# Decode attention of a hybrid decoder step: keys scored in five rounds of four blocks instead of four groups of five, the fold through two banks, score rows turned through a bank of their own

## The reference

```python
H_SB = H_FOX = 5; HEAD_DIM = 64; DEC_BATCH = 8; DEC_SEQ = 8; PAST_LEN = 4096; PAGE_SIZE = 128

# stick-breaking: q (B,T,H,d), k/v (B,S,H,d)
z = (jnp.einsum('bthd,bshd->bhts', qb, k) * scale).astype(F32)
mask = k_pos[None, :] < pb[:, None]
ln1m = jnp.where(mask, jax.nn.log_sigmoid(-z), 0.0)
rc = lax.cumsum(ln1m, axis=3, reverse=True)
excl = jnp.concatenate([rc[..., 1:], jnp.zeros_like(rc[..., :1])], axis=-1)
a = jnp.where(mask, jnp.exp(jax.nn.log_sigmoid(z) + excl), 0.0)
out = jnp.einsum('bhts,bshd->bthd', a, v)

# forgetting attention
s = (jnp.einsum('bthd,bshd->bhts', qb, k) * scale).astype(F32)
s = s + c_q - c_k                                  # cumulative log forget
p = jax.nn.softmax(jnp.where(mask, s, -jnp.inf), axis=-1)
out = jnp.einsum('bhts,bshd->bthd', p, v)

# the past keys and values come out of paged pools
g = pool[page_table]                               # 32 pages of 128 rows per sequence
```

## Time and profile before

| | |
|---|---|
| median of three runs | 3724.05 us |
| the profiled execution | 3717.23 us, of which the traced span is 3715.7 us |
| PE busy in the span | 3302.2 us (89%) |
| DVE, ACT, POOL busy | 1365.7, 937.0, 596.1 us |
| mean granted TensorE clock | 0.912 of full speed |
| scoring matmuls (L1043) | 896 + 384 instructions, 40 per sequence over 32 sequences |
| key loads of 160 KB issued by SP in decode | 248 + 240 per kind |
| value loads of 160 KB issued by POOL | 480 per kind |

### The profile page before, as it was taken

The page is one execution under the profiler, slowest core; times in us unless marked ns, Lnnn a source line. Parts: engine busy times, 40 slices in busy tenths (PEclk is TensorE's granted clock), DMA queues, the critical chain, the costliest instruction groups (busy, mean ns, idle before and its releaser), DMA issues. The chain is left out here.

```text
span 3715.7 us, 67414 instructions
## 1 busy us (share of the span) xinstructions
PE 3302.2 (89%) x25160; PEld 2100.0 (57%) x25160; DVE 1365.7 (37%) x3002; ACT 937.0 (25%) x1682; POOL 596.1 (16%) x1090
## 2 busy tenths in 40 slices
PE   6999999888899878789989999888889997887998
PEld 4566666555576645444445566655556674554443
DVE  3235055444242534412133151664432244442121
ACT  2012122343122433212020122334322253331110
POOL 0000000144200024410000000003540101542000
PEclk9999955899998899989999999889999997998999
DMA  5011100588411179821021111028871204985102
GB/s 173 18 38 45 44 1 1 172 296 289 151 42 62 35 243 299 289 91 50 29 95 34 32 35 38 21 93 266 293 242 44 75 1 151 310 290 191 55 30 71
DMA packets 268656, 439.67 MB, mean 118 GB/s; under 512 B 48817, under 2 KB 216402, under 8 KB 268338
## 3 DMA queue, kind: packets, MB, share of 16 engines
q1 hardware_dynamic: 205810, 239.96, 20.2%
q0 software_dynamic: 55744, 189.25, 15.4%
q10 hardware_dynamic: 6912, 7.87, 0.6%
HBM read 410.28 MB, written 26.65 MB: 118 GB/s over the span
## 5 line engine op out<-in xcount | busy, mean ns | idle before, releaser
L794 PE MATMUL ps<-W,xT 128*128 128x320 f32 (+7 forms) x5120 | 1479.0, 464 | 11.5 <-DVEq L442 11.5
L794 PEld LDWEIGHTS ps<-W,xT 128*128 128x128 f32 (+1 forms) x5120 | 854.2, 183 | 583.3 <-issue 288.3
L676 POOL DMA_DIRECT2D branch<-in_cache_sb_v_dram x480 | 258.1, 538 | 703.6 <-issue 662.7
L676 POOL DMA_DIRECT2D branch<-in_cache_fox_v_dram x480 | 258.1, 538 | 599.3 <-issue 557.1
L1426 ACT ACTIVATE branch<-ps 128x512 f32<-128x512 f32 x288 | 165.7, 595 | 384.0 <-PE ps L1021 379.7
L1021 PE MATMUL ps<-C,W 128*128 128x128 f32 x1280 | 197.7, 299 | 72.5 <-DMA W<-in_cache_fox_k_dram 23.8
L934 PE MATMUL ps<-branch 64*128 64x512 f32 (+7 forms) x480 | 243.6, 643 | 19.7 <-POOLq L442 19.7
L1021 PE MATMUL ps<-C,branch 128*128 128x128 f32 x1280 | 190.6, 290 | 59.7 <-DMA branch<-in_cache_fox_k_dram 16.6
L1106 PE MATMUL ps<-branch 128*8 128x64 f32 x9920 | 180.9, 233 | 58.6 <-DMA branch<-in_cache_fox_v_dram 30.9
L1021 PEld LDWEIGHTS ps<-C,W 128*128 128x128 f32 x1280 | 149.8, 150 | 139.8 <-issue 61.6
L1043 PE MATMUL ps<-branch,work 128*32 128x512 f32 x896 | 224.4, 613 | 0.7
(11 more groups left out here) (237 smaller groups left out, 3364.0 us busy)
## 6 DMA issues: line engine op xcount, KB each, us to landing
branch<-in_cache_sb_v_dram POOLq DMA_DIRECT2D x480, 160.0 KB, 4.4
branch<-in_cache_fox_v_dram POOLq DMA_DIRECT2D x480, 160.0 KB, 4.0
W<-in_cache_sb_k_dram SPq DMA_DIRECT2D x248, 160.0 KB, 3.3
W<-in_cache_fox_k_dram SPq DMA_DIRECT2D x248, 160.0 KB, 3.4
branch<-in_cache_sb_k_dram SPq DMA_DIRECT2D x240, 160.0 KB, 4.5
branch<-in_cache_fox_k_dram SPq DMA_DIRECT2D x240, 160.0 KB, 4.2
W<-in_w_in_dram SPq DMA_DIRECT2D x14, 1280.0 KB, 6.3
W<-in_w_in_dram SPq DMA_DIRECT2D x9, 1536.0 KB, 7.1
```

The source lines that it names most:

```text
L676: pool.dma_start(ringV[:, g % 2, p * DA:(p + 1) * DA], cache[L, bass.ds(pg, 1)].rearrange("a s h d -> s (a h d)"))\
L794: ins = pe.matmul(out, src[:, k, t * P:t * P + R], W[i % 2][:, k, a:z], start=(k == 0), stop=(k == kc - 1), **place)
```

## The change

A scoring now takes four blocks, 4r to 4r + 3, all in one bank (2 or 3 by the round's parity), so there are five rounds of scoring and five turns of rows, one for each. All rows are turned through bank 6, each after the drain of the one before it. The fold of sb goes in three parts through banks 5, 7 and 5, and the addition on DVE is in three parts as well; the fox fold uses bank 5 for the maximum and 7 for the spread. DVE takes block 8 also (ACT no longer does). The orders on PE, ACT and DVE are written anew: weigh 3 moves from behind block 7 to behind block 3, weigh 0, 1 and 2 stand as shown below. The loads are not touched.

```diff
 SLOTS = 8
+ROUNDS = BLOCKS // 4
-DVE_BLOCKS = (2, 3, 11, 13, 15, 17, 19)
+DVE_BLOCKS = (2, 3, 8, 11, 13, 15, 17, 19)
+FOLD_BANKS = (5, 7, 5)
...
-                def score(b, g):
+                def score(b, r):
-                    n = 5 * g + 4
+                    n = 4 * r + 3
...
-                    if not is_first(b) or g >= 2:
-                        pe.wait_ge(s["rows_out"], 5 * b + g - (1 if g >= 2 else 0) if g else 5 * b)
-                    if g == 1 and not is_first(b):
-                        pe.wait_ge(s["soft_ready"], b)
-                    for kk in range(5):
-                        bank = 3 if kk == 4 else (5 if g % 2 else 2)
-                        q = 32 * (g if kk == 4 else kk)
-                        ins = pe.matmul(ps[q:q + 32, bank, :], q_now[:, kk, :], kT_d[(5 * g + kk) % SLOTS],
-                                        start=True, stop=True, tile_position=(0, q), skip_group_check=True)
+                    if not is_first(b) or r >= 2:
+                        pe.wait_ge(s["rows_out"], ROUNDS * b + r - 1)
+                    for a in range(4):
+                        n = 4 * r + a
+                        ins = pe.matmul(ps[32 * a:32 * a + 32, 2 + r % 2, :], q_now[:, n % 5, :], kT_d[n % SLOTS],
+                                        start=True, stop=True, tile_position=(0, 32 * a), skip_group_check=True)
...
-                def turn_rows(b, j):
+                def turn_rows(b, r):
+                    pe.wait_ge(s["rows_out"], ROUNDS * b + r + 1)
+                    if not is_first(b) or r >= 1:
+                        pe.wait_ge(s["z_drained"], ROUNDS * b + r)
                     for m in range(4):
-                        ins = pe.transpose(ps[:, 6 + j % 2, m * P:(m + 1) * P],
-                                           z_rows[:, 2 if j == 4 else j % 2, m * P:(m + 1) * P], ident)
+                        ins = pe.transpose(ps[:, 6, m * P:(m + 1) * P], z_rows[:, r % 3, m * P:(m + 1) * P], ident)
...
-                def fold(b):
+                def fold(b, c):
                     if kind == "sb":
                         pe.wait_ge(s["sum_ready"], b + 1)
+                        if not is_first(b) or c == 2:
+                            pe.wait_ge(s["fold_taken"], 3 * b + c - 1 if c else 3 * b)
+                        cols = slice(c * 440, c * 440 + 440)
+                        out = ps[:, FOLD_BANKS[c], 0:440]
+                        pe.matmul(out, const("earlier"), soft[:, cols], start=True, stop=False)
+                        pe.matmul(out, const("negones"), later[:, cols], start=False, stop=True)\
+                            .then_inc(s["expo_ready"], 1)
```

The order on PE:

```diff
                 def sequence(b, before=None, two_before=None):
-                    turn_blocks(b, range(0, 5))
+                    turn_blocks(b, range(0, 4))
+                    if two_before is not None:
+                        weigh(two_before, 3)
+                    turn_blocks(b, range(4, 8))
+                    score(b, 0)
                     if before is not None:
                         fold_first(before)
-                    turn_blocks(b, range(5, 8))
-                    if two_before is not None:
-                        weigh(two_before, 3)
-                    score(b, 0)
-                    turn_blocks(b, range(8, 10))
+                    turn_blocks(b, range(8, 12))
+                    score(b, 1)
                     if before is not None:
-                        fold(before)
-                    turn_blocks(b, range(10, 13))
+                        fold(before, 0)
+                        fold(before, 1)
                     turn_rows(b, 0)
-                    score(b, 1)
-                    turn_blocks(b, range(13, 15))
+                    if before is not None:
+                        fold(before, 2)
+                    turn_blocks(b, range(12, 16))
+                    score(b, 2)
+                    turn_rows(b, 1)
                     if before is not None:
                         weigh(before, 0)
-                    turn_rows(b, 1)
-                    turn_blocks(b, range(15, 18))
-                    score(b, 2)
-                    turn_blocks(b, range(18, 20))
+                    turn_blocks(b, range(16, 20))
+                    score(b, 3)
+                    turn_rows(b, 2)
                     if before is not None:
                         weigh(before, 1)
-                    turn_rows(b, 2)
-                    score(b, 3)
+                    score(b, 4)
                     turn_rows(b, 3)
-                    turn_rows(b, 4)
                     if before is not None:
                         weigh(before, 2)
+                    turn_rows(b, 4)
```

On DVE the addition of the fold and the order:

```diff
                 def exponents(b):
                     if kind == "sb":
-                        dve.wait_ge(s["expo_ready"], b + 1)
-                        z3 = zs.rearrange("p (c n) -> p c n", c=3)
-                        dve.tensor_tensor(z3, z3, ps[:, 5:8, 0:440], ALU.add).then_inc(s["soft_ready"], 1)
+                        for c in range(3):
+                            dve.wait_ge(s["expo_ready"], 3 * b + c + 1)
+                            z3 = zs[:, c * 440:(c + 1) * 440]
+                            ins = dve.tensor_tensor(z3, z3, ps[:, FOLD_BANKS[c], 0:440], ALU.add)
+                            ins.then_inc(s["fold_taken"], 1)
+                        dve.wait_ge(s["fold_taken"], 3 * b + 3)
+                        dve.sem_inc(s["soft_ready"], 1)
...
                 def sequence(b, before=None, two_before=None):
...
+                    take_blocks(b, (8, 11))
                     if before is not None:
                         exponents(before)
-                    take_blocks(b, (11,))
                     drain(b, 0)
                     if before is not None:
                         denominators(before)
-                    take_blocks(b, (13,))
+                    take_blocks(b, (13, 15))
                     drain(b, 1)
-                    take_blocks(b, (15, 17, 19))
+                    take_blocks(b, (17, 19))
```

97 lines of the change are left out of this document (42 added, 55 removed).

## The result

The changed kernel takes 4069.14 us (median of 4 runs, 4058.79 to 4073.84) against 3725.84 us for the kernel before beside it (3718.55 to 3730.8). The ratio is 1.0919, with a 95% interval of 1.0889 to 1.0949: 9.2% slower. The direction was forecast, the size was not. I had 3868 us and a range up to 3938.

A forecast was written before the change was run, and what follows sets the result against it. Key and value ring loads outlasting PE's work were taken to bind. Per full sequence 4.1 + 1.4 = 5.5 us, with edge sequences 35.5 per phase, 142 over four, giving 3868 us; range 3785 to 3938.

The forecast's parts named there:

- the rival with values in time: Values of group 2 are there when weigh 2 is reached, only keys bind: 30 us faster, 3694 us; chance 0.09.
- not under 9: Sign against the forecast: it is wrong if weigh 2 follows weigh 0 in under 9 us.
- the edits put at nothing: Row turnings through one bank, drains, copies, score waits and block 8's move to DVE: put at 0 us.
- The price of the scoring: Scoring by four blocks saves PE 2.76 us per sequence, 88 us over 32 sequences.
- what is not in this: Per full sequence, overlap of values 2 and keys 1 loads plus lower granted clock, outside the steps: 1.4 us.
- the upper bound of 4.5: Contention and clock together per sequence: between 0 and 4.5 us (1.5 on each of two landings, 1.5 of clock).
- the heavy rival: Rings bind, with clock and contention on top: 8.6 us more per sequence, 3940 us; chance 0.16.
- steps 2: Block 10 to block 15, which waits for DVE's copy of block 13: reached at 19.7 us (sb), 17.5 us (fox).
- 3: Block 15, score 2, rows 1 and weigh 0 take 3.1 us; weigh 0 ends at 22.8 (sb), 20.6 (fox).
- step 1: Block 4 to block 10: 4 us of work under a 9.5 us key load, a wait of over 5 us.
- the pair that the prediction named: Loads of values 2 and keys 1 start almost together, block 19 ending 2.6 us after weigh 0.
- step 5: Weigh 2 to block 4, with weigh 3 waiting for values: sequence closes at 41.0 us (sb), 38.8 us (fox).

The follow-up runs named there:

- Experiment 1: Changed kernel with weigh 3 moved back behind block 7, nothing else moved; 3954.84 us, ratio 1.0614 to the kernel before.
- Experiment 2: Changed kernel with weigh 3 back behind block 7 and the whole fold ahead of block 10; 3939.38 us, ratio 1.0561.
- Experiment 3: Changed kernel with only weigh 0 moved ahead of block 15 and weigh 2 behind the last turning of rows; median 3985.29 us, no ratio.
- Experiment 4: Changed kernel with both load stretches' order put back, keeping rounds of four, one bank for rows and split fold; 3759.04 us, ratio 1.0062.
- Experiments 6: Kernel before with only its PE order changed: weigh 3 ahead of block 4, fold behind block 11; 3978.6 us, ratio 1.0654.
- 11: Kernel before with only weigh 0 moved from behind block 14 to behind block 19, next to weigh 1; 3871.36 us, ratio 1.0391.
- Experiment 10: Changed kernel with PE, ACT and DVE orders rewritten to keep the loads' stretches long, a rerun in more rounds; 3657.78 us, ratio 0.9816.
- Experiment 9: Changed kernel with POOL holding back the load of value group 1 until block 11 of the next sequence is turned; 3978.68 us, ratio 1.0672.
- experiment 5: Changed kernel with filler matmuls, results unread, on PE ahead of block 10 and ahead of weigh 2; 4057.2 us, ratio 1.0876.
- experiment 12: The kernel of Experiment 9 (changed kernel, value group 1 load held back) profiled again; a single execution of 4051.92 us.

## Why the prediction was wrong in size and right in direction

**Right: what binds.** Two loads whose length PE does not set, and an order that takes work out from under both. Experiments 1 to 4 put the work back and get 310 us of 343 back. Experiments 6 and 11 take the work away from the kernel before and lose 250 and 143 us, without any other part of the change. PE did wait the saved scoring off, as said, and the rival with values in time (3694 us) fell: weigh 2 came 12.1 us after weigh 0, not under 9. Block 15 did wait for DVE's copy, 28 times, 74.5 us in all.

**Right: the edits put at nothing.** Experiment 10 has the scoring by four, the one bank for the rows and the split fold, and is 1.8% faster than the kernel before. The price of the scoring was a little high: 2.4 us per sequence by its measured rounds, not 2.76.

**Wrong: "what is not in this", 1.4 us for contention and clock together.** Measured it is 8.6 us per full sequence, nearly twice the upper bound of 4.5 that I gave it; the heavy rival, with 8.6 us more than before in all, had not enough either, since the mean full sequence is 12.7 us longer. The 8.6 us are 2.1 for the keys' load, 2.0 for the values' load, some 3.2 for the clock, 0.8 for steps 2 and 3 reckoned too short at full clock, and 0.5 behind weigh 2. So two terms of the sum itself, both loads, were too small beside the 1.4.

- *The keys' load, 9.5 us in step 1, took 11.6.* The prediction took 9.5 from fox in the kernel before, where the mean over full sequences is 9.8 and POOL had its own times. It looked for contention between values 2 and keys 1, and missed the pair that the moved line makes: weigh 2 and weigh 3 now both start in the 8.6 us ahead of the end of block 4, so that SP's keys 2 and 3 are released together with two groups of values. Experiment 9 shows it most directly, since only the start of one load moves in it: the stretch falls to 8.0 us and the kernel by 90 us, 3.8 us for each of 24 full sequences. Experiment 1 separates the same two loads by moving weigh 3, and shows 8.5. So weigh 3's move did harm twice. It left the stretch that needed cover, and it made that stretch longer.
- *The values' load, 10.1 us in step 2, took 12.1.* Most of this is not new contention: the values were there 11.6 us after weigh 0 in the kernel before as well, and work of about that length hid it. The prediction took the median landing of 4.1 us for the last of eight pages, which takes 5.1, and left out POOL's pause, which it had seen in the earlier trace rows. Only some 0.5 us came with the change. Whether that is the pair that the prediction named, values 2 and keys 1, no run isolates.
- *The clock: some 3.2 of the 4.0 us missing between block 10 and the end of weigh 0.* The next fence has the changed kernel's PE in an sb sequence; two blocks and a scoring that the prediction put at 1.84 us take 922.02 - 918.39 = 3.63 us.

```profile
918.39 1.96 PE L1026 MATMUL ps<-C,W 128*128 128x128 f32 x8 [7.99 <-DMA W<-in_cache_sb_k_dram]
...
922.02 1.00 PE L1071 MATMUL ps<-branch,C 128*128 128x440 f32 x2
...
930.86 0.66 PE L1026 MATMUL ps<-C,branch 128*128 128x128 f32 x4 [1.92 <-DVE W L1935]
931.44 1.38 PE L1043 MATMUL ps<-branch,work 128*32 128x512 f32 x8
932.75 1.11 PE L1054 MATMUL ps<-C,work 128*128 128x128 f32 x4
933.79 2.08 PE L1103 MATMUL ps<-branch 128*8 128x64 f32 x80
935.81 1.09 PE L1026 MATMUL ps<-C,branch 128*128 128x128 f32 x8
```

Behind the second wait, block 15 to the end of weigh 0 is 935.81 - 930.86 = 4.95 us where 3.1 was reckoned; the weighing takes 2.08 us instead of 1.31. Two slow stretches of 1.8 us each, where the prediction had allowed 1.5 us for one. The first comes in all twenty sequences and is worth 2.1 us by experiment 5. The second comes in 13 of 20. Without it the stretch takes 3.5 us and with it 5.0 to 5.9, 4.6 on the mean, so it costs 1.1 us. The other 0.8 us of the 4.0 are there at full clock too (10.9 and 8.2 us against 10.2 and 8.0 in step 2, 3.5 against 3.1 in step 3) and are a miss of those steps. In the fox sequence shown above, block 15 to weigh 0 went at full speed. A third slow stretch, behind weigh 2, lies where step 5 had a wait, as the lower bound in the prediction supposed. In fox the granted clock over the first 4.1 us behind the wait was this (window, in the order of columns given above), which is the lower level of 1.2 GHz all through, and in answer to 0.59 in the earlier trace rows:

```profile
1571.90:1576.00 4.10, 4.05 (x18) 2.06 (x18) 0.69 (x1) 0.75 (x2) 0.00 (x0) 0.50 0.67 228
```

The Trainium skill, TensorE: Matmul & The Clock Gate, on HAM oscillation, was cited for 1.5 us per sequence at most. Its rule that each such wait in a loop sends PE back to the low clock agrees with the trace: 0.50 over the first 3 us behind block 10 in all twenty sequences. What I had wrong is how many of the waits do so. The wait for DVE's copy ahead of block 15 is no wait for a transfer, and the clock fell behind it too, in 4 of 10 sb sequences, where it lasts 1.9 us, and in 9 of 10 in fox, where it lasts 3.4.

How far the clock's cost could be had back is not settled. Experiment 5 got 1.9 us per full sequence, without filler at the second wait, and the kernel gained only 0.3%. Not tried: filler at all three waits.

**The sum, with measured sizes.** Per phase: five full sequences 5 x 12.7 = 63 us; the eighth, to its block 19, 7.7; sequence 1, 9.6 where 3 was forecast; sequence 0, 1.5 longer where 1.5 was to be gained. That is 82 us, four times 327. The span grew by 341.6 us. The other 14 lie between the last block of each phase and its last weighing (36.4 us instead of 32.7 on the mean, where 1 us was forecast). Sequence 0 has neither of the two long waits of the others in full, and why it did not gain its scoring I did not follow.

**The Trainium skill's other rule**, DMA: Bandwidth & Descriptors on the anatomy of a DMA, 2.4 us for a page by its figures: where a queue runs nearly alone the trace comes close, with 2.7 us (experiment 12, keys from SP and values from POOL alike). With two queues at work 4.3 to 4.6 us were measured, and 6.6 for the last page of eight. The prediction was right to set it aside for the sum; here its figure is near what a page takes with little else under way (the shortest single one of POOL in the changed kernel is 2.2 us).

## What to carry to other kernels

Under a ring of buffers, count the work between the release of a half and its next use before and after a change of order, and write beside it which other queue's release now falls into the same microseconds: a moved line that frees one ring just ahead of another can lengthen the load that the compute waits for. Work saved in an engine pays only if the order keeps the stretch under every load as long as the load; here the same edit made the kernel 9.2% slower in one order and 1.8% faster in another. Read a load's length where as many queues run together as the new order will make run together, and take the landing of its last page, not the median.
